# One core, two tuned transformer blocks: the keys of block 1 rotated a step earlier, one queue for the first transfers, and transposes between the halves of an output block

## The chip, the core and the metric

The kernel runs on one core of one Trainium2 chip. Its engines run side by side and wait for each other through semaphores: TensorE (PE in the profile) multiplies matrices, VectorE (DVE) and ScalarE (ACT) work on elements, and SyncE (SP) and ScalarE issue DMA transfers. The metric is the time of one execution on the device in microseconds (us). Times inside an execution are counted from the start of its span.

## What is computed

The input is x, 512 tokens by 1024 columns in 32-bit floats. It goes through two stages of two layers each. A layer of the first stage ("block 1") normalises x, projects it, and runs three branches: A, differential attention of four heads; B, a gated mixing of tokens; C, attention of eight 64-wide heads over dilated windows. The branches are projected, gated, merged and added to x. A layer of the second stage ("block 2") projects x, runs four attention groups of four heads, projects their output, and ends in a feed-forward part.

```python
for l in range(DEPTH):                       # block 1, DEPTH = 2
    h = hybrid_layer(h, positions, l, ...)
...
qc = partial_rope(cq.reshape(B, S, C_HEADS, C_HEAD_DIM), positions)
kc = partial_rope(ck.reshape(B, S, C_HEADS, C_HEAD_DIM), positions)
...
return rmsnorm(h, final_g)                   # then block 2, two layers
```

## The kernel before

**Products.** Activations and weights are split into a rounded high part and a low rest, and each product is three matrix products on TensorE: high by high, low by high, high by low (`mm3`, L590 to L592). Weights come as units of 128 by 1024 through a ring of four slots: SyncE loads a unit (L966), ScalarE casts its high part (L1145), VectorE subtracts to get the low part (L1157), and `split_wait` holds TensorE until that is done.

**Attention in block 1.** The program treats the heads as eight pairs of maps, a = 0 to 7: 0 to 3 (below `N_A`) are branch A, 4 to 7 are branch C. Each has four blocks of 128 queries, qb = 0 to 3. In a step TensorE computes the scores (`scores`, L1281 and L1283), VectorE takes the masked row maximum (`row_max`, L787), ScalarE the exponential (L1552), VectorE divides (`normalise`, L1838 to L1849), TensorE transposes (`transposes`, L1294), ScalarE copies the result, and TensorE multiplies it with the values (`pv`, L1310). The steps are staggered, and between them TensorE fills in the projections of the next head (`fill`). The score banks are shared from block to block, so the scores of a block wait for the row maxima of the block before (`max_ready`). For heads 4, 5 and 6 (`JOINED1`) blocks 0 and 1 are scored and transposed together; block 1 is then called "second" (`second1`), and its row maxima are taken in block 0's step.

**Rotation.** Queries and keys of the next head are rotated by position. SyncE exchanges rows of the copied projection through small DMAs (`exchange1`, L1005), VectorE multiplies and adds (`rotate`, L1800 to L1815) and raises `qk_ready`, and SyncE then places the results with more DMAs (`place1`, L1024 and L1027). `ROTATE1` names the step behind which each rotation stands: queries behind block 0, keys behind block 1.

**Epilogue.** When a head's output is complete, VectorE multiplies it with its gate (`epilogue`). For heads of branch C that is L1869, which reads the output bank and raises `o_out`; the `pv` of the next head's block 0 waits for that. With `finish` the result is also split into parts (`split_y`, L1763 and L1764, which raises `y_ready`); otherwise that is done a step later. The order of all this on VectorE is written out by hand in the loop over a and qb in `vector_block1`.

**The start.** The gain of the first norm is spread over rows on the chip: VectorE makes a diagonal of it (`gain_diagonal`, L1173), TensorE sums its columns with a matrix of ones (`gain_sums`, L1167), VectorE copies the sums (L1635) and scales the first block of x. Products of zeros (L1195) stand between these steps on TensorE. SyncE issues the constants, the gains, and then x and weights in turn; the first block of x goes through ScalarE's queue (L1422).

**The tail of block 2's attention.** Steps are numbered 0 to 31. From `TAIL` = 27 on no projections are left to fill in, and steps 29 and 30 (`OUT_FILL`) each do the last token block of a unit of the output projection (`out_block`, six products) ahead of the transposes of the step before (`between`, L2038).

Of the kernel before, what the change touches and what calls it, by code (L numbers as in the profile page):

```python
# [30 lines left out]
ALU = mybir.AluOpType  # L31
# [118 lines left out]
def program(nc, x_in, pos_in, const_in, mask_in, swa_in, rope2_in, col_in, w_in, row1_in,  # L150
            row2_in, out):
    ctx = ExitStack()
    with ctx:
# [478 lines left out]
            tile_columns(pe, e, n, 0, 0, 1)  # L632
            tile_columns(pe, e, n + 1, 1, 0, 1)

        def tok_block(n, j, tb, kts, st_hi, st_lo, banks=TOK):

            wh = hi_of(n).rearrange("p (k c) -> p k c", c=SEQ)
            wl = lo_of(n).rearrange("p (k c) -> p k c", c=SEQ)
            cols = slice(tb * P, (tb + 1) * P)
            for k in range(2 * j, min(2 * j + 2, kts)):  # L640
                last = mm3(banks[tb][:, :], st_hi[:, k, cols], st_lo[:, k, cols],
                           wh[:, k - 2 * j, :], wl[:, k - 2 * j, :], k == 0, k == kts - 1)
            return last
# [310 lines left out]
        def sync_program(sp):  # L954
# [28 lines left out]
            sp.dma_start(const[:, 0:2 * P], const_in[:, 0:2 * P]).then_inc(ident_loaded, 16)  # L983
            sp.dma_start(colp[:, 0:P1_SUBLN], col_in[0, :, 0:P1_SUBLN]).then_inc(norm_loaded, 16)
            for tb in range(NB):
                if tb:
                    sp.dma_start(x[:, tb, :], x_in[tb * P:(tb + 1) * P, :]).then_inc(x_loaded[tb], 16)
                if tb < 2:
                    load(tb)
            load(2)  # L990
# [170 lines left out]

        def gain_sums(pe):

            diag = gain_diag[:, :, :].rearrange("p k c -> p (k c)")
            for c in range(2):
                pe.wait_ge(gain_diag_ready, c + 1)
                nc.tensor.matmul(T[c][:, :], ones, diag[:, SEQ * c:SEQ * (c + 1)], start=True, stop=True).then_inc(gain_summed, 1)  # L1167

        def gain_diagonal(dve):

            dve.wait_ge(norm_loaded, 16)
            for c in range(2):
                nc.vector.tensor_tensor(gain_diag[:, 4 * c:4 * c + 4, :], ident.unsqueeze(1).to_broadcast([P, 4, P]),  # L1173
                                        colp[:, P1_NORM + 4 * c:P1_NORM + 4 * c + 4].unsqueeze(2).to_broadcast([P, 4, P]),
                                        ALU.mult).then_inc(gain_diag_ready, 1)


        def tensor_block1(pe, layer):
# [11 lines left out]

            if layer == 0:

                def zero_products(n, cols=SEQ):
                    for _ in range(n):
                        nc.tensor.matmul(O[:, 0:cols], ytmp[:, 0:P], ytmp[:, 0:cols], start=True, stop=True)  # L1195

                pe.wait_ge(zeros_ready, 1)
                zero_products(1)
                zero_products(1, SEQ // 2)
                pe.wait_ge(ident_loaded, 16)  # L1200
                gain_sums(pe)
                zero_products(1)
                entry_transpose(pe, e, 0, hn[0], (0,))
                zero_products(2)
                v_block(0, 0)
                for tb in range(1, NB):
                    entry_transpose(pe, e, tb, hn[tb], (0,))
                    if tb == 2:
                        pe.wait_ge(gain_ready, 2)
                    v_block(1, tb - 1)  # L1210
                    if tb == NB - 1:
                        entry_transpose(pe, e, 0, hn[0], (1,))
                    v_block(0, tb)
                entry_transpose(pe, e, 1, hn[1], (1,))
                v_block(1, NB - 1)
                for tb in range(NB):
                    if tb == 0:
                        entry_transpose(pe, e, 2, hn[2], (1,))
                    v_block(2, tb)
                    if tb == 0:  # L1220
                        entry_transpose(pe, e, 3, hn[3], (1,))
                    v_block(3, tb)
            else:
                for tb in range(2):
                    v_block(0, tb)
                    v_block(1, tb)
                entry_transpose(pe, e, 3, hn_of(e, 3))
                for tb in range(2, NB):
                    v_block(0, tb)
                    v_block(1, tb)  # L1230
                for tb in range(NB):
                    v_block(2, tb)
                    v_block(3, tb)
# [184 lines left out]

        def scalar_block1(act, st, layer):
            at, n0, e = Counts(names, layer), layer * B1_UNITS, ENTRY1[layer]  # L1420
            if layer == 0:
                act.dma_start(x[:, 0, :], x_in[0:P, :]).then_inc(x_loaded[0], 16)  # L1422
            nc.scalar.preload_act_table_set("natural_log_exp_and_others")
            def lam_exps():
                act.wait_ge(lam_exp, at(lam_exp, 1))
# [240 lines left out]
        def vector_block1(dve, st, layer):  # L1666
# [212 lines left out]
            for a in range(N_ATT):  # L1879
                for qb in range(NB):  # L1880
                    if not second1(a, qb):
                        for own in GROUPS1[GROUP1_AT[a, qb]]:
                            row_max(*own, 0)
                            row_max(*own, 1)
                    before = steps_back(a, qb, 1)
                    if before and fill_of(*before) == ("z", before[0]):
                        silu_z(before[0])
                    if (a, qb) == (0, 0):
                        split_to(dve, n0 + B1_HEADS + 6)
                    elif fill_of(*before):  # L1890
                        split_to(dve, n0 + head_unit(*fill_of(*before)) + 3)
                    if second1(a, qb):
                        normalise(a, qb)
                    if before in ROTATE1:
                        rotate(*ROTATE1[before])
                    if (a, qb) in EPILOGUE1:
                        if qb:
                            dve.wait_ge(qk_ready, at(qk_ready, 2 * a + 3))
                        epilogue(EPILOGUE1[a, qb])
                    elif qb == (2 if a in JOINED1 else 1) and a > N_A:  # L1900
                        epilogue(a - 1, False)
                    elif qb == 3 and a > N_A:
                        split_y(8 + a - 1 - N_A)
                        dve.wait_ge(y_ready, at(y_ready, 4 + a))
                    if not second1(a, qb):
                        normalise(a, qb)
                    if qb == (2 if a in JOINED1 else 1) and 1 <= a <= N_A:
                        split_squares(a - 1)
# [27 lines left out]
        def tensor_block2(pe, layer):  # L1936
# [185 lines left out]
                    v_transpose(name)  # L2122


            def out_block(j, tb):
                return tok_block(n0 + B2_WO + j, j, tb, KD, act_hi, act_lo, WO_BANKS[0])

            first_tiles(pe, e, n0, (at(tile_out[0], 0), at(tile_out[1], 0)))
            part(FIRST[2], range(KD))
# [1 line left out]
            for i, group in enumerate(GROUPS):  # L2131
# [17 lines left out]
                if step in OUT_FILL:  # L2149
                    j = OUT_FILL[step]  # L2150
                    split_wait(pe, n0 + B2_WO + j)
                    pe.wait_ge(y_ready, at(y_ready, 4))
                    pe.wait_ge(r_out, at(r_out, R2["fv1"] + 1))
                    out_block(j, NB - 1)
                if step and not beside:
                    between(step - 1)
                fill(step, 1)
                if step in LATE:
                    late_work(LATE[step])
# [1020 lines left out]
```

## Time and profile before

| | us |
|---|---|
| median of 3 runs | 2323.68 |
| lowest and highest run | 2322.32, 2325.24 |
| profiled execution, own time | 2325.3 |
| its span | 2323.5 |
| TensorE busy in it | 2308.4 |
| VectorE busy | 1481.2 |
| ScalarE busy | 978.6 |

The span goes from the first to the last instruction of the profiled execution. Busy time of TensorE is the time in which a matrix product was under way by the profile, whose product ends are modelled.

### The profile page before, as it was taken

To read this page: it belongs to the slowest core of one execution; us is meant where nothing else is said; L and a number is where in the kernel's file an instruction comes from. 1 tells how busy PE (TensorE), PEld (TensorE's weight loads), DVE (VectorE), ACT (ScalarE), POOL (GpSimd) and SP (SyncE) were. 2 spreads that over 40 slices of the span, in tenths; PEclk is the share of its full clock that TensorE was granted. 3 is DMA by queue.
4 is the path that set the end of the run, shared out by engine and by line. 5 is a ranking of instruction groups with operands and counts; after the bars stand their busy time and mean duration, and the time that the engine had idled before them with its cause. 6 is when DMAs were issued, how large, how long until landed. Compare 5 with 4: busy or idle time off the path is not lost.

```text
span 2323.5 us, 30126 instructions
## 1 busy us (share of the span) xinstructions
PE 2308.4 (99%) x11442; PEld 1881.9 (81%) x11442; DVE 1481.2 (64%) x2781; ACT 978.6 (42%) x1811; POOL 0.2 (0%) x4
## 2 busy tenths in 40 slices
PE   9999999999999999999999999999999999999998
PEld 6888888888888878888877788888887768888887
DVE  6788763435478784444587668566567777658565
ACT  5356542223446553222567543232336764323222
POOL 0000000000000000000000000000000000000000
PEclk9999999999999999999999999999999999999999
DMA  4333334333243333233221133314313112422322
GB/s 167 107 105 105 104 96 112 92 99 100 84 117 109 97 103 114 93 100 117 65 88 55 56 127 102 127 55 145 118 37 97 55 46 100 145 82 91 127 64 99
DMA packets 74766, 226.84 MB, mean 98 GB/s; under 512 B 15296, under 2 KB 16192, under 8 KB 73856
## 3 DMA queue, kind: packets, MB, share of 16 engines
q1 hardware_dynamic: 74336, 224.14, 30.9%
q8 instruction: 92, 1.51, 0.3%
q10 hardware_dynamic: 288, 0.79, 0.1%
q14 instruction: 50, 0.41, 0.1%
HBM read 205.36 MB, written 2.10 MB: 89 GB/s over the span
## 4 chain that ended last, share of the span: by engine, by line
PE 96%; DVE 2%; ACT 1%; issue 0%; DMA 0%; DVEq 0%; SPq 0%
PE bank L590 25%; PE bank L592 25%; PE bank L591 25%; PE bank L2235 2%; PE bank L2237 2%; PE bank L2236 2%; PE bank L1310 2%; PE bank L2054 1%; PE bank L2013 1%; PE bank L1294 1%; PE bank L2038 1%; PE bank L524 1%; PE bank L1283 1%; PE bank L1281 1%; PE bank L2067 1%; PE bank L2096 0%
## 5 line engine op out<-in xcount | busy, mean ns | idle before, releaser
L590 PE MATMUL bank<-h_hi,w_hi 128*128 128x512 f32 x1984 | 784.7, 396 | 0.7 <-DVE sz L1769 0.3
L592 PE MATMUL bank<-h_lo,w_hi 128*128 128x512 f32 x1984 | 773.4, 390 | 0.0
L591 PE MATMUL bank<-h_hi,w_lo 128*128 128x512 f32 x1984 | 773.0, 390 | 0.0
L1157 DVE TENSOR_TENSOR w_lo<-raw_w,w_hi 128x1024 fp32r<-128x1024 f32 x314 | 378.9, 1221 | 97.4 <-ACT w_hi L1145 94.1
L590 PEld LDWEIGHTS bank<-h_hi,w_hi 128*128 128x128 f32 x1984 | 372.7, 188 | 82.5 <-issue 8.3
L592 PEld LDWEIGHTS bank<-h_lo,w_hi 128*128 128x128 f32 x1984 | 372.4, 188 | 79.8
L591 PEld LDWEIGHTS bank<-h_hi,w_lo 128*128 128x128 f32 x1984 | 372.9, 188 | 72.1
L1145 ACT ACTIVATE w_hi<-raw_w 128x1024 fp32r<-128x1024 f32 x314 | 327.6, 1054 | 159.5 <-DMA raw_w<-w_dram 159.1
L2472 ACT ACTIVATE nrm<-bank 128x512 f32<-128x512 f32 x44 | 26.4, 599 | 288.4 <-PE bank L592 288.4
L1611 ACT ACTIVATE ext<-bank 128x512 f32<-128x512 f32 x48 | 28.7, 598 | 274.3 <-PE bank L592 274.3
L1918 DVE TENSOR_TENSOR rope_a<-ext,bank 128x512 f32<-128x512 f32 x32 | 22.0, 688 | 165.8 <-PE bank L592 109.7
L1552 ACT ACTIVATE prob<-prob,small 128x128 f32<-128x128 f32 (+3 forms) x128 | 70.8, 556 | 65.0 <-DVE small L787 65.0
L2235 PE MATMUL bank<-seven_hi,y_hi 128*128 128x512 f32 x252 | 98.1, 389 | 0.0
L2236 PE MATMUL bank<-seven_hi,y_lo 128*128 128x512 f32 x252 | 98.0, 389 | 0.0
L2866 DVE TENSOR_TENSOR ytmp<-nrm,bank 128x512 f32<-128x512 f32 x26 | 17.9, 688 | 117.0 <-PE bank L592 116.9
L590 PE MATMUL bank<-act_hi,w_hi 128*128 128x512 f32 x212 | 83.0, 392 | 0.0
L592 PE MATMUL bank<-act_lo,w_hi 128*128 128x512 f32 x212 | 82.6, 389 | 0.0
L591 PE MATMUL bank<-act_hi,w_lo 128*128 128x512 f32 x212 | 82.5, 389 | 0.0
L787 DVE CUSTOM_DVE_ANT_0 prob<-bank,causal 128x128 f32<-128x128 f32 (+3 forms) x112 | 49.5, 479 | 35.3 <-PE bank L1283 19.9
L2866 DVE TENSOR_TENSOR y_raw<-nrm,bank 128x512 f32<-128x512 f32 x18 | 12.4, 688 | 91.5 <-PE bank L592 91.5
L2934 DVE SCALAR_TENSOR_TENSOR x<-x,bank 128x512 f32<-128x512 f32 x84 | 54.7, 681 | 20.7 <-PE bank L2237 20.7
L1567 ACT ACTIVATE pT<-bank 128x384 f32<-128x384 f32 (+3 forms) x84 | 36.8, 470 | 58.9 <-PE bank L1294 58.9
(372 smaller groups left out, 3504.6 us busy)
## 6 DMA issues: line engine op xcount, KB each, us to landing
raw_w<-w_dram SPq DMA_DIRECT2D x312, 512.0 KB, 3.6
down_raw<-w_dram SPq DMA_DIRECT2D x36, 512.0 KB, 4.5
extra_raw<-w_dram SPq DMA_DIRECT2D x10, 512.0 KB, 4.6
k_lo<-k_lo SPq DMA_DIRECT2D x32, 128.0 KB, 2.3
ln_row<-row_dram SPq DMA_DIRECT2D x4, 1024.0 KB, 6.6
last_raw<-w_dram SPq DMA_DIRECT2D x8, 512.0 KB, 4.6
rowp<-row_dram SPq DMA_DIRECT2D x2, 1024.0 KB, 11.9
rot_t<-raw_t SPq DMA_DIRECT2D x128, 16.0 KB
```

What stands on the lines that cost most here:

```text
L590: nc.tensor.matmul(dst, lh, rh, start=start, stop=False)
L591: nc.tensor.matmul(dst, ll, rh, start=False, stop=False)
L592: return nc.tensor.matmul(dst, lh, rl, start=False, stop=stop)
L787: return nc.vector.tensor_tensor_reduce(out=to, in0=bank, in1=mask, scale=-1.0, scalar=3.0e38, op0=ALU.add, op1=ALU.min, accum_out=low)
L1145: nc.scalar.activation(hi_of(u), raw_of(u), ACT.Copy).then_inc(hi_cast, 1)
L1157: nc.vector.tensor_tensor(lo_of(u), raw_of(u), hi_of(u).bitcast(F32), ALU.subtract) \
L1310: last = nc.tensor.matmul(O[rows, cols], vs[a % 2][:, b, rows], pT[ti1(a, qb, m) % 2][:, of + b * P:of + (b + 1) * P], start=(b == 0), sto ...
L1552: nc.scalar.activation(prob[m][:, own], prob[m][:, own], ACT.Exp, scale=-1.0, bias=small[:, 24 + 2 * qb + m:25 + 2 * qb + m], accum_out=sm ...
L2235: nc.tensor.matmul(bank[t][:, :], y_hi[:, p, a, y], high, start=begin, stop=False, skip_group_check=True)
L2236: nc.tensor.matmul(bank[t][:, :], y_lo[:, p, a, y], high, start=False, stop=False, skip_group_check=True)
L2237: made = nc.tensor.matmul(bank[t][:, :], y_hi[:, p, a, y], low, start=False, stop=p == PAIRS - 1, skip_group_check=True)
L2934: nc.vector.scalar_tensor_tensor(out=part, in0=part, scalar=scale, in1=bank[t][:, :], op0=ALU.mult, op1=sign).then_inc(down_added, 1)
```

## The change

In the first three functions the start is rewritten: SyncE issues all four blocks of x, the gain diagonal is one instruction, and the products of zeros are two before and two behind the sums. In `vector_block1`, for heads 4 to 6, the rotation of the next head's keys is done in block 1's step right behind that of its queries; in block 2's step the epilogue of the head before (heads 5 and 6) stands directly ahead of the normalisation, behind a wait on `y_ready`; the epilogue of head 3 in head 5's block 1 waits for the keys' rotation instead of the queries'. In `tensor_block2` the output block of step 29 is done in two halves with the transposes between them.

```diff
--- before.py
+++ after.py
@@ -632,12 +632,12 @@
             tile_columns(pe, e, n, 0, 0, 1)
             tile_columns(pe, e, n + 1, 1, 0, 1)
 
-        def tok_block(n, j, tb, kts, st_hi, st_lo, banks=TOK):
+        def tok_block(n, j, tb, kts, st_hi, st_lo, banks=TOK, halves=(0, 1)):
 
             wh = hi_of(n).rearrange("p (k c) -> p k c", c=SEQ)
             wl = lo_of(n).rearrange("p (k c) -> p k c", c=SEQ)
             cols = slice(tb * P, (tb + 1) * P)
-            for k in range(2 * j, min(2 * j + 2, kts)):
+            for k in [2 * j + half for half in halves if 2 * j + half < kts]:
                 last = mm3(banks[tb][:, :], st_hi[:, k, cols], st_lo[:, k, cols],
                            wh[:, k - 2 * j, :], wl[:, k - 2 * j, :], k == 0, k == kts - 1)
             return last
@@ -983,8 +983,7 @@
             sp.dma_start(const[:, 0:2 * P], const_in[:, 0:2 * P]).then_inc(ident_loaded, 16)
             sp.dma_start(colp[:, 0:P1_SUBLN], col_in[0, :, 0:P1_SUBLN]).then_inc(norm_loaded, 16)
             for tb in range(NB):
-                if tb:
-                    sp.dma_start(x[:, tb, :], x_in[tb * P:(tb + 1) * P, :]).then_inc(x_loaded[tb], 16)
+                sp.dma_start(x[:, tb, :], x_in[tb * P:(tb + 1) * P, :]).then_inc(x_loaded[tb], 16)
                 if tb < 2:
                     load(tb)
             load(2)
@@ -1161,18 +1160,17 @@
 
         def gain_sums(pe):
 
+            pe.wait_ge(gain_diag_ready, 1)
             diag = gain_diag[:, :, :].rearrange("p k c -> p (k c)")
             for c in range(2):
-                pe.wait_ge(gain_diag_ready, c + 1)
                 nc.tensor.matmul(T[c][:, :], ones, diag[:, SEQ * c:SEQ * (c + 1)], start=True, stop=True).then_inc(gain_summed, 1)
 
         def gain_diagonal(dve):
 
             dve.wait_ge(norm_loaded, 16)
-            for c in range(2):
-                nc.vector.tensor_tensor(gain_diag[:, 4 * c:4 * c + 4, :], ident.unsqueeze(1).to_broadcast([P, 4, P]),
-                                        colp[:, P1_NORM + 4 * c:P1_NORM + 4 * c + 4].unsqueeze(2).to_broadcast([P, 4, P]),
-                                        ALU.mult).then_inc(gain_diag_ready, 1)
+            nc.vector.tensor_tensor(gain_diag[:, :, :], ident.unsqueeze(1).to_broadcast([P, KD, P]),
+                                    colp[:, P1_NORM:P1_NORM + KD].unsqueeze(2).to_broadcast([P, KD, P]), ALU.mult) \
+              .then_inc(gain_diag_ready, 1)
 
 
         def tensor_block1(pe, layer):
@@ -1190,16 +1188,14 @@
 
             if layer == 0:
 
-                def zero_products(n, cols=SEQ):
+                def zero_products(n):
                     for _ in range(n):
-                        nc.tensor.matmul(O[:, 0:cols], ytmp[:, 0:P], ytmp[:, 0:cols], start=True, stop=True)
+                        nc.tensor.matmul(O[:, :], ytmp[:, 0:P], ytmp[:, :], start=True, stop=True)
 
                 pe.wait_ge(zeros_ready, 1)
-                zero_products(1)
-                zero_products(1, SEQ // 2)
+                zero_products(2)
                 pe.wait_ge(ident_loaded, 16)
                 gain_sums(pe)
-                zero_products(1)
                 entry_transpose(pe, e, 0, hn[0], (0,))
                 zero_products(2)
                 v_block(0, 0)
@@ -1418,8 +1414,6 @@
 
         def scalar_block1(act, st, layer):
             at, n0, e = Counts(names, layer), layer * B1_UNITS, ENTRY1[layer]
-            if layer == 0:
-                act.dma_start(x[:, 0, :], x_in[0:P, :]).then_inc(x_loaded[0], 16)
             nc.scalar.preload_act_table_set("natural_log_exp_and_others")
             def lam_exps():
                 act.wait_ge(lam_exp, at(lam_exp, 1))
@@ -1889,20 +1883,25 @@
                         split_to(dve, n0 + B1_HEADS + 6)
                     elif fill_of(*before):
                         split_to(dve, n0 + head_unit(*fill_of(*before)) + 3)
+                    if qb == 2 and a in JOINED1 and a > N_A:
+                        dve.wait_ge(y_ready, at(y_ready, 3 + a))
+                        epilogue(a - 1, False)
+                    if qb in (1, 2) and a in JOINED1:
+                        normalise(a, qb)
+                    if before in ROTATE1 and not (a in JOINED1 and qb == 2):
+                        rotate(*ROTATE1[before])
                     if second1(a, qb):
-                        normalise(a, qb)
-                    if before in ROTATE1:
-                        rotate(*ROTATE1[before])
+                        rotate(*ROTATE1[a, qb])
                     if (a, qb) in EPILOGUE1:
                         if qb:
-                            dve.wait_ge(qk_ready, at(qk_ready, 2 * a + 3))
+                            dve.wait_ge(qk_ready, at(qk_ready, 2 * a + 4))
                         epilogue(EPILOGUE1[a, qb])
-                    elif qb == (2 if a in JOINED1 else 1) and a > N_A:
+                    elif qb == 1 and a > N_A and a not in JOINED1:
                         epilogue(a - 1, False)
                     elif qb == 3 and a > N_A:
                         split_y(8 + a - 1 - N_A)
                         dve.wait_ge(y_ready, at(y_ready, 4 + a))
-                    if not second1(a, qb):
+                    if qb not in (1, 2) or a not in JOINED1:
                         normalise(a, qb)
                     if qb == (2 if a in JOINED1 else 1) and 1 <= a <= N_A:
                         split_squares(a - 1)
@@ -2122,8 +2121,8 @@
                     v_transpose(name)
 
 
-            def out_block(j, tb):
-                return tok_block(n0 + B2_WO + j, j, tb, KD, act_hi, act_lo, WO_BANKS[0])
+            def out_block(j, tb, halves=(0, 1)):
+                return tok_block(n0 + B2_WO + j, j, tb, KD, act_hi, act_lo, WO_BANKS[0], halves)
 
             first_tiles(pe, e, n0, (at(tile_out[0], 0), at(tile_out[1], 0)))
             part(FIRST[2], range(KD))
@@ -2151,9 +2150,11 @@
                     split_wait(pe, n0 + B2_WO + j)
                     pe.wait_ge(y_ready, at(y_ready, 4))
                     pe.wait_ge(r_out, at(r_out, R2["fv1"] + 1))
-                    out_block(j, NB - 1)
+                    out_block(j, NB - 1, (0,) if step == TAIL + 2 else (0, 1))
                 if step and not beside:
                     between(step - 1)
+                if step == TAIL + 2:
+                    out_block(OUT_FILL[step], NB - 1, (1,))
                 fill(step, 1)
                 if step in LATE:
                     late_work(LATE[step])
```

## Rows read from the trace of the kernel before

**Rows 1.** The page of the profile, busy time of each engine.
```profile
PE 2308.4 (99%) x11442; PEld 1881.9 (81%) x11442; DVE 1481.2 (64%) x2781; ACT 978.6 (42%) x1811; POOL 0.2 (0%) x4
```

**Rows 2.** Waits of PE, whole span: us in total, times, longest us.
```profile
PE bank L1310 <- issue: 2.6, 2, 1.3
PE bank L1167 <- DVE gain_diag L1173: 1.5, 1, 1.5
...
PE bank L590 <- DVE w_lo L1157: 1.0, 2, 0.8
PE bank L2054 <- ACT pT L2355: 0.5, 2, 0.3
```

**Rows 3.** Timeline of the first 17 us: start, us busy, engine, line, operation.
```profile
1.45 2.93 PE L1195 MATMUL bank<-ytmp 128*128 128x512 f32 x4 [1.45 <-DVE ytmp L1718]
1.63 0.43 SPq L966 DMA_DIRECT2D raw_w<-w_dram  x1
...
5.05 1.29 DVE L1173 TENSOR_TENSOR gain_diag<-const,colp 128x512 f32<-128x512 f32 x2 [3.66 <-DMA colp<-col_dram]
...
5.89 3.75 PE L1167 MATMUL bank<-gain_diag,const 128*128 128x512 f32 x4 [1.52 <-DVE gain_diag L1173]
...
6.19 0.20 ACT L547 ACTIVATE small<-small 128x1 f32<-128x1 f32 x1
...
11.99 1.91 PE L1195 MATMUL bank<-ytmp 128*128 128x512 f32 x4
...
13.59 0.53 PE L590 MATMUL bank<-w_hi,h_hi 128*128 128x512 f32 x1
...
16.58 0.50 PE L590 MATMUL bank<-w_hi,h_hi 128*128 128x512 f32 x1 [0.76 <-DVE w_lo L1157]
```

**Rows 4.** DMA issues by line: count, KB each, us from issue to landing.
```profile
k_lo<-k_lo SPq DMA_DIRECT2D x32, 128.0 KB, 2.3
...
x<-x_dram ACTq DMA_DIRECT2D x1, 512.0 KB, 4.0
...
const<-const_dram SPq DMA_DIRECT2D x1, 128.0 KB, 3.5
...
colp<-col_dram SPq DMA_DIRECT2D x1, 4.0 KB, 3.8
```

**Rows 5.** Timeline of DVE, head 5 of layer 0, blocks 1 and 2.
```profile
270.29 0.69 DVE L1864 TENSOR_TENSOR rope_a<-ext,nrm 128x512 f32<-128x512 f32 x1
...
272.87 0.55 DVE L787 CUSTOM_DVE_ANT_0 prob<-bank,mult 128x384 f32<-128x384 f32 x1
...
273.82 0.08 DVE L787 DVE_READ_ACCUMULATOR2_ANT small<- 128x1 f32 x1
...
274.96 0.68 DVE L1800 TENSOR_TENSOR rope_a<-raw_t,cos 128x512 f32<-128x512 f32 x1
...
279.24 0.69 DVE L1869 SCALAR_TENSOR_TENSOR ytmp<-bank,sz 128x512 f32<-128x512 f32 x1
```

**Rows 6.** Timeline of PE around the scores of head 5, block 3.
```profile
274.96 0.39 PE L1281 MATMUL bank<-ext_r,q_two 128*128 128x512 f32 x1
...
280.03 0.88 PE L1310 MATMUL bank<-pT,vs 128*64 128x128 f32 x12 [1.28 <-issue]
281.10 0.88 PE L1294 MATMUL bank<-const,pn 128*128 128x128 f32 x6 [0.19 <-DVE pn L1849]
```

**Rows 7.** Timeline of SyncE: the exchange that feeds the keys of head 6.
```profile
264.87 2.64 SPq L1005 DMA_DIRECT2D rot_t<-raw_t  x4
```

**Rows 8.** Timeline of DVE, last row maxima of heads 4 and 6.
```profile
238.17 0.08 DVE L787 DVE_READ_ACCUMULATOR2_ANT small<- 128x1 f32 x1
...
300.41 0.08 DVE L787 DVE_READ_ACCUMULATOR2_ANT small<- 128x1 f32 x1
```

**Rows 9.** Timeline of PE, scores of heads 4 and 6, block 3.
```profile
244.61 0.71 PE L1281 MATMUL bank<-act_lo,act_hi 128*128 128x512 f32 x2
...
306.78 0.61 PE L1281 MATMUL bank<-act_lo,act_hi 128*128 128x512 f32 x2
```

## Prediction

> **What bounds the kernel now.** I read the page first: TensorE is busy 99% of the span [rows 1], so only its own work and its own waits count; VectorE and ScalarE matter where TensorE waits for them. The view of waits, restricted to TensorE, then lists all it lost to others: about 8 us in 2323.5 [rows 2]. That is the ceiling of what any reordering can give, unless instructions of TensorE go away too. Three of these waits lie near the edits: twice 1.3 us in front of L1310 (the product with the values), once 1.5 us in front of the gain sums, and twice about 0.3 us in front of L2054. The view blames the first on "issue"; the code tells more. The product for head 5, block 0, waits for `o_out`, which VectorE raises in `epilogue(4, False)`, L1869, at 279.24 plus 0.69, and TensorE goes on at 280.03 [rows 5, 6]. So it is VectorE's order of work in head 5, and as it is counted twice, it is there in both layers of block 1. Last I read the timelines of VectorE and TensorE around the three edits.
>
> **Edit 1: the keys' rotation moves up.** For heads 4, 5 and 6 `rotate("k", a+1)` leaves block 2's step, where it stood behind the row maxima, and goes directly behind `rotate("q", a+1)` in block 1's step, ahead of those maxima. Its price: it starts at 274.96 and what follows it at 279.24, so 4.28 us of VectorE [rows 5]. Nothing is added or removed; what was between the two places gets 4.28 us later, what came after stays where it was, since VectorE has no gap there.
>
> Head 5 first. Behind the queries comes `epilogue(3)` from 270.29, then the row maxima of block 2 from 272.87 to 273.90 [rows 5]. The new order is keys 270.29 to 274.57, epilogue, maxima from 277.15 to 278.18. Are the keys there by 270.29? Their exchange is issued from 264.87 to 267.51 [rows 7]; with the 2.3 us that a larger transfer inside SBUF needs [rows 4] it has landed by 269.8. So they are, with 0.5 us to spare. Queued on VectorE behind the maxima are the weight split, `epilogue(4, False)` and the normalisation; waiting for the maxima are ScalarE's exponentials and, what matters, TensorE's scores of block 3, which reuse the bank. Those scores start at 274.96 [rows 6], 1.06 us after the maxima were done. Now the first of the four may start at 277.75 and the second, which needs the other map's maximum, at about 278.24 instead of 275.18: 3.06 us late.
>
> Given back: TensorE then does its fill and comes to the product with the values. Without the old wait it would have been there at 280.03 - 1.28 = 278.75; now it is there at 278.75 + 3.06 = 281.81. `epilogue(4, False)` still begins at 279.24: it lost 4.28 us of rotation in front of it, and got the 4.28 us by which the maxima and the split are later. So its wait of 1.28 is gone, and the 0.19 in front of L1294 too [rows 6], but they are gone because TensorE arrives late. Net: 3.06 - 1.28 - 0.19 = 1.6, and about 0.1 less because TensorE's normal step from L1310 to L1294 is shorter than the one that held the wait. I take +1.5 us a layer, +3.0 us in both. The normalisation's own place, now behind the epilogue as before, doesn't move.
>
> Heads 4 and 6 pay nothing. Their last maxima end at 238.25 and 300.49 [rows 8]; 4.28 later is 242.5 and 304.8, and TensorE wants them at 244.61 and 306.78 [rows 9], some 2 us after. The new wait on `y_ready` ahead of `epilogue(a - 1, False)` is met by VectorE's own split, two steps of work earlier: nothing. SyncE, whose placements wait for the rotated keys, issues them and the weight loads behind them 4.28 us sooner, which no TensorE wait asks for: nothing. Without that spare in heads 4 and 6 each would cost what it lacked, up to 4.28 us. Bounds of edit 1: if the maxima were overtaken as written but the keys land 1 us late, +5 us in both layers; if TensorE didn't wait for the maxima, the two waits of 1.28 and 0.19 would fall, -2.9 us.
>
> A fall of TensorE's clock is the danger of such a wait. The longest wait so far after the start is 1.3 us [rows 2], and the work behind it runs on at the warm pace; no row shows a wait of 2.8 us. The Trainium skill (TensorE: Matmul & The Clock Gate, Part 1) says that a TensorE left idle falls to half its clock and must be busy again to get it back. By the sum above it stays warm; by that rule a fall is possible, and it is the rival below.
>
> **Edit 2: the start.** SyncE issues the first rows of x as its third transfer, where the first weights were issued at 1.63 [rows 3], instead of ScalarE through a queue of its own. The gain diagonal is one instruction of 1024 columns instead of two of 512, so the first sum waits for all of it. TensorE's filler is two full products ahead of the sums instead of one and a half, and the full one behind the sums is gone. So half a product less in all.
>
> Now: filler 1.45 to 4.38, then a wait, because the diagonal begins only at 5.05, when the 4 KB of gains land 3.8 us after their issue; sums from 5.89, 3.75 us [rows 3, 4]. Those 4 KB queue behind 128 KB of constants that took 3.5 us while the 512 KB of x ran beside them on ScalarE's queue; 128 KB alone need 2.3 [rows 4]. Without x beside them I take the gains 1.2 us earlier (bounds 0 and 1.5), so the diagonal runs from 3.85 to 5.1, its 1.29 us unsplit. The filler, 2.93 times 2 / 1.5 = 3.9 us, ends at 5.35. So the diagonal is hidden, and the sums start at 5.35, 0.5 earlier. x is issued at most 1.63 us later, so its statistics, done at 6.39 [rows 3], are done by 8.0 at the latest; they are needed together with the gain row, which is there only behind the first sum (5.35 + 1.87 = 7.2) and its copy: nothing. Behind the sums a cold product (half of 3.75, so 1.9; 1.7 without its tail) is missing: the transposes come 0.5 + 1.7 = 2.2 us earlier.
>
> Not all of it stays. Four passes took 3.75 us at 5.89 and 1.91 at 11.99 [rows 3]: the array ran at 1.2 GHz and from about 12 at 2.4 GHz. The two products behind the transposes, warm until now, start near 9.8 and run cold until 12, which gives back 1.1. So the first weights' products begin at 12.5 instead of 13.59. But ScalarE and VectorE, which feed the second unit, are the whole 2.2 ahead, and the 0.8 us for its split at 16.58 [rows 2, 3] goes. I take -1.6 us, between 1.1 and 2.0 to 2.2. Bounds: if the gains land no earlier, the diagonal ends at 6.35 and the sums start 0.5 late; the start then gives only -0.4. If the clock rises one cold stretch earlier, as TensorE no longer pauses at 4.38, -2.8. If it rises 3 us later, +0.5.
>
> The Trainium skill (DMA: Bandwidth & Descriptors, Issuing engines are not separate DMA queues) has it that transfers from several engines share the same DMA engines and interleave, and that a second queue saves only issue time. The landing of the 128 KB at 3.5 instead of 2.3 agrees with it. By that rule alone the order of landing changes, not the total.
>
> **Edit 3: block 2's last head.** In step 29 the transposes stand between two halves (three products each) of an output block instead of behind it. TensorE does the same instructions; the transposes come under a microsecond earlier, but no wait for them is listed. The wait that is listed there, L2054 for `pT`, 0.3 us at the longest [rows 2], is for the next block's transposes, which stay behind a whole output block. So nothing is gained; one more change between kinds of product I price at 0.1 us a layer, +0.2 us (bounds -0.5, all of that wait in both layers, and +0.5).
>
> **The sum.** +3.0 - 1.6 + 0.2 = +1.6 us. Against the profiled span 2323.5 that is 2325.1. The profiled execution's own time, 2325.3, is the top of the three runs, whose median is 2323.68; I put the change on the median: 2325.3 us, +0.07%. That is inside 0.2% (4.6 us), about what a measurement of this kernel can tell from no change.
>
> **The rivals.**
> - *The clock falls in the new wait (slower).* For: a wait of some 2.8 us where none over 1.3 was. Against: work resumes each time, and the first score comes in the middle of it. Price: the cold stretch at the start lasted 10.5 us, so up to 5.2 lost in each layer, 10.5 in both: 2335.8. It decides from 3 us of loss in the two layers together on, which is 3 cold microseconds in each: +1.6 + 3 = +4.6. Chance 0.06.
> - *The start gives nothing or less.* The gains land no earlier or the clock rises later: -0.4 to +0.5 in place of -1.6, so 2326.5 to 2327.4. Chance 0.17.
> - *The scores don't wait (faster).* If the maxima were not the last thing that block 3's scores wait for, only the old waits would fall: -2.9 - 1.6 = -4.5, 2319.2. Against: TensorE passes there 1.06 us behind the maxima, and 4.28 is more than that. Chance 0.07.
> - *Keys late.* The exchange lands after 270.3 and VectorE waits: each microsecond costs both layers one, 2327.3. Chance 0.05.
>
> **How the numbers follow.** The forecast has 0.65. Its own range, from the bounds of the start and of edit 3, is 2323.5 to 2327.5; with the start's and the keys' rivals and half of the faster one the range is 2321.5 to 2328.5, and the clock's rival and the other half are left out. Faster by over 0.2% only if the third rival meets a warm start: 0.05. Slower by over 0.2%: the clock's rival and the late keys together with a poor start, 0.09. Within: 0.86.
>
> **What the new profile would show.** Edit 1: a wait of nearly 3 us at L1281 for L787 in head 5 of both layers, L1310's 1.3 gone, L1869 still about 279. Edit 2: no wait for the gain diagonal, L590's first product near 12.5. Edit 3: L2054's wait as before. I am wrong if L1281 shows no wait, if heads 4 or 6 show one, or if TensorE's passes take twice as long after 278.

## The result, and the profile after

The changed kernel takes 2327.85 us (median of 15 runs, 2326.23 to 2329.76), the kernel before 2323.68 us (15 runs): ratio 1.0017, 95% interval 1.0010 to 1.0024. That is 4.2 us more: inside the 0.2% that the prediction named and inside its range, but the interval lies above 1, and +1.6 was forecast. Its profiled execution took 2327.3 us, with a span of 2325.5.

The busy time of the engines on the page, and then the view of TensorE's waits (us in total, times, longest us), both of the changed kernel:

```profile
PE 2308.7 (99%) x11440; PEld 1882.3 (81%) x11440; DVE 1481.2 (64%) x2780; ACT 977.3 (42%) x1811; POOL 0.2 (0%) x4
```

```profile
PE bank L1277 <- DVE small L787: 5.4, 2, 2.7
PE bank L1193 <- DVE ytmp L1712: 1.4, 1, 1.4
PE bank L524 <- DVE hn L553: 1.2, 1, 1.2
PE bank L590 <- DVE w_lo L1156: 0.8, 1, 0.8
PE bank L2053 <- ACT pT L2356: 0.5, 2, 0.3
...
```

Line numbers have moved: L1277 are the scores, L1306 the product with the values, L1290 the transposes, L1166 the gain sums. Against [rows 2], the waits for `o_out` (2.6 in all) and for the gain diagonal (1.5) are gone. In their place stand twice 2.7 us in front of the scores, for the row maxima, and once 1.2 in front of the first transposes, for the normalised x. VectorE in head 5 of layer 0, from its timeline, shows where the 2.7 come from:

```profile
265.88 0.69 DVE L1794 TENSOR_TENSOR rope_a<-raw_t,cos 128x512 f32<-128x512 f32 x1
...
270.17 0.69 DVE L1858 TENSOR_TENSOR rope_a<-ext,nrm 128x512 f32<-128x512 f32 x1
...
272.75 0.55 DVE L787 CUSTOM_DVE_ANT_0 prob<-bank,mult 128x384 f32<-128x384 f32 x1
...
273.71 0.08 DVE L787 DVE_READ_ACCUMULATOR2_ANT small<- 128x1 f32 x1
...
274.84 0.68 DVE L1863 SCALAR_TENSOR_TENSOR ytmp<-bank,sz 128x512 f32<-128x512 f32 x1
```

The keys' rotation from 265.88 and `epilogue(3)` from 270.17 now both stand ahead of the row maxima. TensorE meanwhile, from its timeline (start, duration, idle time before it in brackets):

```profile
270.26 0.39 PE L592 MATMUL bank<-h_lo,w_hi 128*128 128x512 f32 x1
273.37 0.50 PE L1277 MATMUL bank<-ext_r,q_two 128*128 128x512 f32 x1 [2.71 <-DVE small L787]
273.85 0.50 PE L1277 MATMUL bank<-ext_r,ext_r 128*128 128x512 f32 x1
...
274.92 0.63 PE L590 MATMUL bank<-h_hi,w_hi 128*128 128x512 f32 x1
275.35 0.63 PE L591 MATMUL bank<-h_hi,w_lo 128*128 128x512 f32 x1
...
277.83 0.39 PE L591 MATMUL bank<-h_hi,w_lo 128*128 128x512 f32 x1
278.06 0.40 PE L592 MATMUL bank<-h_lo,w_hi 128*128 128x512 f32 x1
...
279.08 0.88 PE L1306 MATMUL bank<-pT,vs 128*64 128x128 f32 x12
279.88 0.87 PE L1290 MATMUL bank<-const,pn 128*128 128x128 f32 x6
280.51 0.47 PE L590 MATMUL bank<-h_hi,w_hi 128*128 128x512 f32 x1
```

The same two places in the kernel before, ahead of the scores and behind the transposes:

```profile
274.73 0.39 PE L592 MATMUL bank<-h_lo,w_hi 128*128 128x512 f32 x1
...
281.73 0.47 PE L590 MATMUL bank<-h_hi,w_hi 128*128 128x512 f32 x1
```

Two things are to be seen. The wait is there, as long as foretold, and L1306 and L1290 no longer wait. But the products behind the wait start 0.43 us apart (274.92 and 275.35) instead of the 0.23 between 277.83 and 278.06. The view by windows names the reason. Its columns are the window, its length, busy time and instructions of PE, PEld, DVE, ACT and POOL, then the granted clock of TensorE as a share of full speed, the DMA share and GB/s. First layer 0, then the same place in layer 1:

```profile
262.00:271.50 9.50, 8.65 (x53) 6.76 (x51) 9.09 (x16) 0.90 (x2) 0.00 (x0) 1.00 0.35 94
271.50:274.40 2.90, 1.03 (x3) 0.69 (x4) 2.83 (x8) 1.05 (x3) 0.00 (x0) 0.98 0.97 184
274.40:277.80 3.40, 3.40 (x9) 2.62 (x8) 3.15 (x8) 2.72 (x7) 0.00 (x0) 0.51 0.35 140
277.80:281.00 3.20, 3.20 (x26) 2.46 (x25) 3.13 (x7) 1.77 (x6) 0.00 (x0) 1.00 0.00 0
...
827.00:830.40 3.40, 3.40 (x8) 2.53 (x9) 3.15 (x8) 3.40 (x8) 0.00 (x0) 0.54 0.61 179
830.40:833.80 3.40, 3.40 (x25) 2.53 (x25) 3.37 (x8) 1.55 (x5) 0.00 (x0) 0.96 0.00 0
```

From 274.4 to 277.8 the granted clock is 0.51 of full speed: 1.2 GHz instead of 2.4. Lost there: 3.40 x (1 - 0.51) = 1.7 us. In layer 1 it is 3.40 x (0.46 + 0.04) = 1.7 again. The Trainium skill (TensorE: Matmul & The Clock Gate, Part 1) says that an idle TensorE falls to half its clock and returns to full after sustained work; the trace agrees, with 0.51 behind an idle time of 2.71 us.

The start of the changed kernel, from the timeline of its first 17 us:

```profile
1.45 3.56 PE L1193 MATMUL bank<-ytmp 128*128 128x512 f32 x4 [1.45 <-DVE ytmp L1712]
...
3.14 1.22 DVE L1171 TENSOR_TENSOR gain_diag<-const,colp 128x1024 f32<-128x1024 f32 x1 [1.75 <-DMA colp<-col_dram]
...
4.84 1.88 PE L1166 MATMUL bank<-gain_diag,const 128*128 128x512 f32 x4
...
7.12 0.75 DVE L553 SCALAR_TENSOR_TENSOR hn<-x,small,gain_row 128x512 f32<-128x512 f32 x1 [0.53 <-ACT small L547]
7.92 0.66 PE L524 MATMUL bank<-const,hn 128*128 128x128 f32 x4 [1.20 <-DVE hn L553]
...
8.42 1.88 PE L1193 MATMUL bank<-ytmp 128*128 128x512 f32 x4
...
9.99 0.54 PE L590 MATMUL bank<-w_hi,h_hi 128*128 128x512 f32 x1
...
12.98 0.50 PE L590 MATMUL bank<-w_hi,h_hi 128*128 128x512 f32 x1 [0.77 <-DVE w_lo L1156]
```

Against [rows 3] the gains are there 1.9 us earlier (3.14 for 5.05), the four passes of the sums take 1.88 instead of 3.75, and the first weights are multiplied at 9.99 instead of 13.59. The DMA view shows why the gains came:

```profile
const<-const_dram SPq DMA_DIRECT2D x1, 128.0 KB, 2.1
colp<-col_dram SPq DMA_DIRECT2D x1, 4.0 KB, 1.9
```

Both landed late in [rows 4], 3.5 and 3.8 us after their issue, with x beside them. The Trainium skill (DMA: Bandwidth & Descriptors, Issuing engines are not separate DMA queues) says that transfers of several engines interleave on the same DMA engines; these rows agree.

### The profile page after: what moved, and what is told of

It is laid out like the page before. It is cut to its first block, busy times and chain, and to the rows that moved or that the text cites. A ratio compares the mean times of both kernels' runs of the same rounds, so it can differ in the third digit from the quotient of the medians.

```text
span 2325.5 us, 30121 instructions
## 1 busy us (share of the span) xinstructions
PE 2308.7 (99%) x11440; PEld 1882.3 (81%) x11440; DVE 1481.2 (64%) x2780; ACT 977.3 (42%) x1811; POOL 0.2 (0%) x4
## 3 DMA queue, kind: packets, MB, share of 16 engines
q8 instruction: 92, 1.51, 0.3%
## 4 chain that ended last, share of the span: by engine, by line
PE 96%; DVE 2%; ACT 1%; issue 0%; DMA 0%; DVEq 0%; SPq 0%
PE bank L590 25%; PE bank L592 25%; PE bank L591 25%; PE bank L2236 2%; PE bank L2238 2%; PE bank L2237 2%; PE bank L1306 2%; PE bank L2053 1%; PE bank L2012 1%; PE bank L1290 1%; PE bank L2037 1%; PE bank L524 1%; PE bank L1279 1%; PE bank L1277 1%; PE bank L2066 1%; PE bank L2095 0%
## 5 line engine op out<-in xcount | busy, mean ns | idle before, releaser
L590 PE MATMUL bank<-h_hi,w_hi 128*128 128x512 f32 x1984 | 785.7, 396 | 0.2
L592 PE MATMUL bank<-h_lo,w_hi 128*128 128x512 f32 x1984 | 774.1, 390 | 0.0
L590 PEld LDWEIGHTS bank<-h_hi,w_hi 128*128 128x128 f32 x1984 | 373.4, 188 | 82.2 <-issue 7.6
L592 PEld LDWEIGHTS bank<-h_lo,w_hi 128*128 128x128 f32 x1984 | 372.9, 188 | 79.8
L590 PE MATMUL bank<-act_hi,w_hi 128*128 128x512 f32 x212 | 83.0, 392 | 0.0
L592 PE MATMUL bank<-act_lo,w_hi 128*128 128x512 f32 x212 | 82.6, 389 | 0.0
```

Source lines behind the costliest of these rows:

```text
L590: nc.tensor.matmul(dst, lh, rh, start=start, stop=False)
L592: return nc.tensor.matmul(dst, lh, rl, start=False, stop=stop)
```

## The experiments

**Theory.** Edit 1 costs 1.5 us a layer through the late row maxima and 1.7 through the clock that falls in that wait, some 6.4 in all; edit 2 gives back 2 to 4, almost all of it through the queue of the first x; edit 3 is nothing. **Rivals.** The loss is the wait alone (+3.0) and something else makes up the rest; or whatever is moved on VectorE in head 5, another step becomes late by as much. Ratios below are to the kernel before on the same chip; its medians there were 2324.78 (e1, e3, e4, e5), 2324.76 (e2, e6, e8, e10) and 2324.16 (e9, e11, e12).

**One edit at a time.** e1_rotation is the kernel before with edit 1 alone:

```diff
+                    if qb == 2 and a in JOINED1 and a > N_A:
+                        dve.wait_ge(y_ready, at(y_ready, 3 + a))
+                        epilogue(a - 1, False)
...
                     if second1(a, qb):
-                        normalise(a, qb)
-                    if before in ROTATE1:
-                        rotate(*ROTATE1[before])
+                        rotate(*ROTATE1[a, qb])
...
```

> Edit 1 alone. Theory (TensorE waits for the late row maxima, and its clock falls behind each such wait): +1.5 us of wait and +1.7 us of half clock in each layer, +6.3 us in all, a wait of 2.7 us at L1277 twice, and granted clock near 0.5 for some 3.4 us behind it in both layers. Rival (the wait alone; the fall belongs to something else in the changed kernel): +3.0 us and a granted clock of 1.0 throughout.

Measured: 2331.16 us, ratio 1.0028 (1.0017 to 1.0040), +6.4. The rival's +3.0 is out, since the interval begins at +4.0. There are only six runs, and they fall apart: two took 2328.5 and 2328.7, four 2331.0 to 2332.2, the longest of them the profiled one. What sets the two groups apart isn't known. The clock in layer 1, in the view by windows, stayed low longer than in the changed kernel. By these rows 3.40 x (0.11 + 0.50 + 0.39) = 3.4 us of clock are gone, but some of that fell in the wait itself, in the first of these windows, where TensorE was busy for only 0.67 us, so it cost less (2.6 us, worked out below):

```profile
827.00:830.40 3.40, 0.67 (x4) 0.25 (x2) 3.26 (x8) 0.10 (x1) 0.00 (x0) 0.89 0.60 141
830.40:833.80 3.40, 3.40 (x8) 2.63 (x9) 3.15 (x8) 3.39 (x8) 0.00 (x0) 0.50 0.56 176
833.80:837.20 3.40, 3.40 (x11) 2.37 (x12) 3.37 (x8) 1.52 (x4) 0.00 (x0) 0.61 0.02 5
```

e2_start is edit 2 alone, e8_xqueue only its move of x to SyncE's queue, e10_diagonal only its merged diagonal and filler, e3_tail edit 3 alone:

```diff
 e8:
-                if tb:
-                    sp.dma_start(x[:, tb, :], ...
+                sp.dma_start(x[:, tb, :], ...
...
-            if layer == 0:
-                act.dma_start(x[:, 0, :], ...
 e10:
...
-            for c in range(2):
-                nc.vector.tensor_tensor(gain_diag[:, 4 * c:4 * c + 4, :], ...
+            nc.vector.tensor_tensor(gain_diag[:, :, :], ...
...
-                zero_products(1)
-                zero_products(1, SEQ // 2)
+                zero_products(2)
...
-                zero_products(1)
 e3:
...
-                    out_block(j, NB - 1)
+                    out_block(j, NB - 1, (0,) if step == TAIL + 2 else (0, 1))
...
+                if step == TAIL + 2:
+                    out_block(OUT_FILL[step], NB - 1, (1,))
```

> Edit 2 alone (both of its parts). Theory: the gains land earlier, so TensorE doesn't pause behind its first products and its clock rises earlier: -2 to -4 us, the sum of edit 1's +6.3 and this being the +4.2 measured. Rival (the gain of the start is eaten by later waits for weights): 0.

> Of edit 2 only the queue: x's first block goes through SyncE; the diagonal stays in two halves, and the filler as before. Theory: the gains land about 1.9 us earlier, as in the changed kernel, the wait of 1.5 us for the diagonal goes, and most of the start's gain is here: -1.5 to -3 us. Rival (the merge and the filler carry it): 0.

> Of edit 2 only the diagonal in one instruction and the filler moved ahead of the sums; x's first block stays on ScalarE's queue. Theory: the gains land at 4.95 as before, so the whole diagonal is ready 0.6 us later than its first half was; with the product behind the sums gone the first weights' products come at about the same time: -0.4, within 1 us of nothing. Rival: the start's gain is here, -2 us or more.

> Edit 3 alone. Theory: the wait for pT stays, and one more turn between kinds of product costs 0.1 to 0.2 us a layer: +0.2 to +0.4 us, not told from nothing. Rival (the earlier transposes shorten the wait at L2054): -0.5 us and no wait there.

Measured: e2 2322.47 (0.9993, interval 0.9984 to 1.0002), -2.3; e8 2322.53 (0.9992, 0.9983 to 1.0001), -2.2; e10 2323.72 (0.9998, 0.9989 to 1.0007), -1.0; e3 2324.51 (1.0002, 0.9993 to 1.0010; the median is 0.3 lower). All four intervals reach 1, those of e2 and e8 only just. But all 11 runs of e8 (2321.82 to 2323.30) are faster than 27 of the 33 of the kernel before (2321.80 to 2326.95), and in the traces the gains land 1.9 us after their issue in e8 and 3.7 in e10, where TensorE still waits 1.1 us for the diagonal. So the start's gain comes with the move of x; the diagonal and the tail can't be told from nothing. The fastest runs of the kernel before are no slower than e8's, so what goes is mostly the slow executions. The move changes two things at once: x's first rows are issued by SyncE instead of ScalarE, and at 1.64 us, behind the gains, instead of 0.74, ahead of them. Which of the two counts wasn't tried. The timeline of e8 shows the mechanism with the two old diagonal instructions still in place (L1172 makes the diagonal, L1166 sums it):

```profile
3.13 1.29 DVE L1172 TENSOR_TENSOR gain_diag<-const,colp 128x512 f32<-128x512 f32 x2 [1.74 <-DMA colp<-col_dram]
4.17 1.99 PE L1166 MATMUL bank<-gain_diag,const 128*128 128x512 f32 x4
```

Against the median the start gives 2.3, though the two traces of before and after stand 3.6 apart at the first weights' product. The kernel before's profiled execution was a late one. The start of that product in all profiles, us:

| start | profiles | first weights' product |
|---|---|---|
| old | before | 13.59 |
| old | e1, e3, e4, e5, e6, e12 | 12.82, 12.09, 12.74, 12.95, 12.85, 12.14 (mean with before 12.74) |
| new | after, e2, e9, e11 | 9.99, 10.12, 10.52, 10.57 (mean 10.30) |
| x moved only | e8 | 9.83 |
| diagonal and filler only | e10 | 12.02 |

The means of old and new are 2.4 apart (2.3 without the late one), as e2's median is.

**Is it the wait or the clock?** e4_filled12 and e5_filled6 are e1 with 12 and 6 products ahead of the scores of head 5's block 3. They write a bank that is free there, and nothing reads what they write, so TensorE is kept busy through the wait, or through half of it, while the maxima stay as late as they are:

```diff
+                if (a, qb) == (5, 3):
+                    pe.wait_ge(r_out, at(r_out, R1["sum", 3] + 1))
+                    for _ in range(12):      # 6 in e5
+                        nc.tensor.matmul(R[:, :], h_hi[:, 0, 0:P], h_hi[:, 0, :], start=True, stop=True)
                 if banks1(a, qb) is S:
```

> Edit 1, and ahead of the scores of head 5, block 3, twelve extra products of 512 columns into a bank that is free there and that nobody reads (2.7 us of TensorE at full clock, as long as the wait). Theory: the scores start when they did with edit 1, but the clock doesn't fall: +3.0 us against the kernel before, 3.3 less than edit 1 alone, though TensorE has more to do. Rival (idle TensorE isn't the cause of the fall, or the loss is in VectorE's order alone): the same time as edit 1 alone, or up to 5 us more as the products are added to it.

> As the run with twelve extra products, with six (1.4 us), so that a wait of about 1.4 us stays. Theory: a wait as long as the one that the kernel before had at L1310 (1.28 us) leaves the clock up: +3.0 us against the kernel before. Rival (any new wait there drops the clock): about +6.

Measured: e4 2327.57 (1.0015, 1.0006 to 1.0024) and e5 2327.54 (1.0013, 1.0004 to 1.0022), both +2.8, where e1 has +6.4. So the useless products cost nothing that the wait didn't cost already, and save 3.6, the price of the clock. By windows, e4 has no slow stretch (two windows of 4.0 and 3.4 us):

```profile
273.00:277.00 4.00, 4.00 (x17) 2.81 (x16) 3.86 (x10) 0.70 (x3) 0.00 (x0) 1.00 0.70 159
277.00:280.40 3.40, 3.40 (x15) 2.54 (x14) 3.15 (x8) 2.80 (x7) 0.00 (x0) 1.00 0.41 145
```

In e5 half the wait is left, and the clock stays up behind it (its waits, then its windows):

```profile
PE bank L1281 <- DVE small L787: 2.7, 2, 1.4
```

```profile
273.00:276.60 3.60, 2.28 (x11) 1.53 (x9) 3.46 (x8) 0.00 (x0) 0.00 (x0) 1.00 0.62 167
276.60:280.00 3.40, 3.37 (x14) 2.58 (x15) 3.20 (x7) 3.39 (x8) 0.00 (x0) 1.00 0.57 186
```

e9_all_filled puts e4's 12 products into the changed kernel in full.

> The changed kernel in full with 12 products that nothing reads ahead of the scores of block 3 in head 5, so that TensorE works through the time in which it waited. Theory (1.7 us a layer of the loss is the clock that falls in the wait): 3 to 3.5 us faster than the changed kernel, 2324.0 to 2325, with the granted clock at 2.4 GHz throughout head 5, although 2.7 us a layer are spent on useless products. Rival (the wait alone is the loss): level with the changed kernel, 2327.5 to 2328.

Measured: 2325.32 (1.0005, 0.9996 to 1.0014), +1.2 against the kernel before where the changed kernel has +4.2: 3.0 us gained by adding products, though its time lies just above the range stated. The rival, that the wait alone is the loss, is out here too.

**Which order is right?** e6_epilogue leaves the keys' rotation where it was in the kernel before, and in head 5, block 2, puts `epilogue(4, False)` and the normalisation ahead of it:

```diff
+                    early = (a, qb) == (N_A + 1, 2)
+                    if early:
+                        dve.wait_ge(y_ready, at(y_ready, 3 + a))
+                        epilogue(a - 1, False)
+                        normalise(a, qb)
                     if before in ROTATE1:
                         rotate(*ROTATE1[before])
...
```

> The kernel before, with only head 5's block 2 changed: directly behind the row maxima and the weight split come the epilogue of head 4 and the normalisation, and the keys' rotation behind both. Theory: the scores don't wait, the wait of 1.28 us at L1310 goes without a new one, the clock stays up: -1.5 us a layer, -2.9 us in all. Rival (the rotation delays something further on, such as the maxima of block 3): 0 or more.

Measured: 2324.92 (1.0001, 0.9992 to 1.0010): no gain, a miss. The old waits are gone from its list, and this one has come, 1.55 us in front of head 6's first scores in layer 0 and 1.51 in layer 1 (the granted clock behind both is 1.00; in layer 0 from 285.0 to 288.4):

```profile
PE bank L1281 <- DMA k_lo<-k_lo: 3.1, 2, 1.6
```

The rotation now ends late, and SyncE places the keys late: its issues at L1027, from the queue's timeline, stand at 281.24 and 282.52 instead of 279.75 and 281.03 in the kernel before. So the keys' rotation has a due time of its own, hardly later than where it stood. Head 5 has three due times on one engine: the maxima of block 2, `epilogue(4)`, and the keys. The changed kernel meets the last two and misses the first; e6 meets the first two. One piece has no due time so near: `epilogue(3)`, 2.6 us, which in both kernels stands ahead of the maxima. e11_epi3 is the changed kernel with it moved behind them, and with the weight split behind the normalisation; e12_epi3_alone has the same order with edit 1 only (old start and tail):

```diff
-                    elif fill_of(*before):
+                    elif fill_of(*before) and (a, qb) != (N_A + 1, 2):
...
+                    if (a, qb) == (N_A + 1, 2):
+                        dve.wait_ge(qk_ready, at(qk_ready, 2 * a + 4))
+                        epilogue(N_A - 1)
                     if qb == 2 and a in JOINED1 and a > N_A:
                         dve.wait_ge(y_ready, at(y_ready, 3 + a))
                         epilogue(a - 1, False)
                     if qb in (1, 2) and a in JOINED1:
                         normalise(a, qb)
+                    if (a, qb) == (N_A + 1, 2):
+                        split_to(dve, n0 + head_unit(*fill_of(*before)) + 3)
...
-                    if (a, qb) in EPILOGUE1:
+                    if (a, qb) in EPILOGUE1 and a != N_A + 1:
```

> The changed kernel in full, but in head 5 the epilogue of head 3 (2.6 us of VectorE) stands behind the row maxima of block 2 instead of ahead of them, and the weight split behind the normalisation. Theory (what costs is the row maxima being late in front of the scores of block 3, plus the clock that falls in that wait; the keys' early rotation itself is wanted): the maxima end about 2.6 us sooner, the wait of 2.7 us shrinks to about 0.5, the clock stays at 2.4 GHz, epilogue(4) ends at about the time at which the product with the values wants it; 3 to 4 us a layer less than the changed kernel, so 2320 to 2322, which is 2 to 4 us under the kernel before. The placement of head 6's keys, which took the gain back when the epilogue alone was moved up in the kernel before, is in time here, since the keys are rotated early. Rival (whatever is moved in head 5, another step becomes late by the same amount): a new wait in head 5 or 6 and a time no better than that of the kernel before with the new start, 2322.5.

> The same order of head 5, but in the kernel before with edit 1 only (old start, old tail). Theory: about 0.5 to 0.9 us a layer faster than the kernel before, since the old waits of 1.28 and 0.19 us go and waits of 0.3 to 0.5 stay, so 0 to 2 us under the kernel before, and some 7 us under edit 1 alone as it was made. Rival (another step becomes late): level with the kernel before or above it.

Measured: e11 2320.59 (0.9982, 0.9974 to 0.9991), 3.6 under the kernel before and the fastest of all; e12 2322.16 (0.9992, 0.9983 to 1.0000), -2.0, where e1, which differs from it only in this order, has +6.4. In e11's list no wait of head 5 or 6 is left. Its TensorE around the same place, and the window with the scores:

```profile
271.27 0.39 PE L592 MATMUL bank<-h_lo,w_hi 128*128 128x512 f32 x1
271.80 0.50 PE L1277 MATMUL bank<-ext_r,q_two 128*128 128x512 f32 x1
272.28 0.50 PE L1277 MATMUL bank<-ext_r,ext_r 128*128 128x512 f32 x1
...
275.88 0.88 PE L1306 MATMUL bank<-pT,vs 128*64 128x128 f32 x12
276.70 0.88 PE L1290 MATMUL bank<-const,pn 128*128 128x128 f32 x6
```

```profile
270.00:274.00 4.00, 3.85 (x17) 2.65 (x16) 3.87 (x9) 2.22 (x7) 0.00 (x0) 1.00 0.65 198
```

The scores start 0.53 and then 0.48 apart where products start 0.23 apart: half a microsecond is lost, against 1.28 + 0.19 in [rows 6], and the clock stays at 1.00. The keys are placed from 271.68, and the first scores of head 6 start at 280.54.

One measure takes the wait and the clock in head 5 together. It is worked out from the timelines: the time from the start of the last product ahead of the scores of block 3 (L592; 274.73 in the kernel before) to that of the first behind the transposes (L590; 281.73), us.

| kernel | layer 0 | layer 1 |
|---|---|---|
| before | 7.00 | 6.99 |
| changed kernel | 10.25 | 10.13 |
| e1 | 9.88 | 11.29 |
| e4, e5, e9 | 8.66, 8.65, 8.66 | 8.68, 8.65, 8.65 |
| e11, e12 | 6.06, 6.08 | 6.07, 6.07 |

With the clock up (e4, e5, e9) the late maxima cost 1.7 us a layer. What the changed kernel takes beyond that is the clock: 1.6 and 1.5; in e1 it is 1.2 and 2.6. In e12 the 0.9 us gained in each layer are the whole of its -2.0.

## Why the prediction was right, and where it was not

**Edit 1, the wait: right.** The second score was forecast 3.06 us late. It starts 3.59 us behind the last product ahead of the scores (270.26 to 273.85), where it started 0.45 behind it (274.73 to 275.18): 3.14 late. The old waits fell with it, heads 4 and 6 show none, and the keys were there in time. e4 and e5, where the clock stays up, measure the net: +2.8 for two layers, forecast +3.0; the table above has 1.7 a layer for the 1.5 forecast.

**Edit 1, the clock: the step that failed.** It is the sentence "By the sum above it stays warm", resting on a wait of 1.3 us behind which work ran on at the warm pace. That row said nothing on a wait twice as long. The sum put at nothing a term of 1.7 us a layer by the granted clock, 3.4 in both; by the starts of products it is 3.1, and the filled kernels took away 3.0 (e9) and 3.6 (e4). The sign of being wrong that the prediction named, passes that take twice as long, did appear, behind the wait. The rival had the mechanism and set 3 us as its deciding point, which this reaches, but its price, up to 5.2 a layer, was taken from the start's stretch of 10.5 us. Its chance was put at 0.06 because work resumes each time; work did resume at 273.37, and the clock was down behind it all the same.

**Edit 2: the gain came, its terms were off.** -1.6 was taken, -2.3 measured by the medians; e2's interval, from -3.7 to +0.5, holds both, so it is the traces that tell the terms apart. The gains came 1.9 us earlier, past the upper bound of 1.5. The term "gives back 1.1" was wrong: the clock was up for the sums (1.88 us instead of 3.75), as in the bound named "one cold stretch earlier". In e2 it was the same (1.89), in e11 the sums took 2.94, so how much of them is slow differs from one execution to the next. Against that, the wait for the second unit's split, 0.8 and counted as gone, stayed (0.77). x's statistics, priced at nothing, now hold the first scaling of x for 0.53, and that is part of the 1.20 that the transposes wait. And the anchor was off: the trace read was of a late execution of the old start.

**Edit 3: right,** no change that can be told, with L2053's wait as before.

**The sum.** 3.0 + 3.4 - 2.3 + 0.2 (edit 3 as forecast, too small to measure) = +4.3, measured +4.2. That the number stayed in the range is luck. It passed the forecast's own range, which ended at 2327.5, and lies in the part that was added for two rivals that didn't come; the clock's rival had been left out of it. With the start at -1.6 the sum would have been +5.0, 2328.7, outside. The start's larger gain took 0.7 off a missing term of 3.4.

## What to carry to other kernels

List the due times of everything on an in-order engine before moving one piece: here the piece that was free to move was neither of those that were late. A new wait on TensorE costs its length and can cost a slow stretch behind it; if it can't be removed, products that nothing reads can be cheaper than idleness. Read the start of an execution from several profiles: with the same old start the first weights' product came between 12.09 and 13.59.

## What was not expected of the hardware

- Idle times of 1.35 us (e5) and 1.55 us (e6) left the granted clock at 1.00 behind them in both layers. Those of 2.71 and 2.73 brought it to 0.50 to 0.60 in the windows behind them, in both layers of the changed kernel and of e1. Lengths between were not tried.
- The slow stretch behind the same wait cost 1.2 to 1.6 us in three of these four places and 2.6 in the fourth (e1, layer 1). What decides between the two stays open.
- 4 KB on SyncE's queue landed 3.8 us after their issue when 512 KB had been issued on ScalarE's queue just ahead of them, and 1.9 when those 512 KB came behind them on SyncE's own (e8 and the changed kernel).
